# c @ ada_w moved from TensorE tiles into VectorE sums inside the two feed-forwards

## What is computed

```python
c_act = jax.nn.silu(c)                                  # c: [1, 1024]
for l in range(2):
    mod = c_act @ ada_w[l] + ada_b[l]                   # ada_w[l]: [1024, 6144]
    sh1, sc1, g1 = mod[:, None, 0:D], mod[:, None, D:2*D], mod[:, None, 2*D:3*D]
    sh2, sc2, g2 = ...
    h = rmsnorm(x, norm1_g[l]) * (1.0 + sc1) + sh1
    x = x + g1 * token_mix(h, ...)
    h = rmsnorm(x, norm2_g[l]) * (1.0 + sc2) + sh2
    x = x + g2 * grouped_moe(h, ...)

def swiglu(x, w_in, w_out):                             # the feed-forward of the first block
    a, b = jnp.split(x @ w_in, 2, axis=-1)
    return (jax.nn.silu(a) * b) @ w_out
```

## Time and profile before

| | |
|---|---|
| median of 3 runs | 1691.95 us (1687.12 to 1695.83) |
| the profiled execution: time | 1687.15 us |
| its span, first to last instruction | 1685.4 us |
| PE, DVE, ACT busy | 1537.0, 915.9, 722.9 us (91%, 54%, 43% of the span) |
| mean granted clock | 0.963 |
| chain that ended last | PE 77%, DVE 12%, ACT 5%, DMA 3%, issue 3% |
| DMA over the span | 401.98 MB, 239 GB/s |
| c @ ada_w on PE (L1562) | 768 records, 47.1 us busy |

### The profile page before, as it was taken

How to read it: one execution, slowest core, us unless ns; L and a number is a source line. 1 busy time by engine, 2 the same in 40 slices (tenths; PEclk the granted TensorE clock), 3 DMA queues, 4 the chain that set the end, 5 groups by cost and what they waited for, 6 DMA issues and landing times.

```text
span 1685.4 us, 25947 instructions
## 1 busy us (share of the span) xinstructions
PE 1537.0 (91%) x10264; PEld 1222.2 (73%) x10264; DVE 915.9 (54%) x1408; ACT 722.9 (43%) x1056; POOL 39.5 (2%) x95
## 2 busy tenths in 40 slices
PE   6999999899999999999599999979998959999996
PEld 6999987479998886777476655559788747665563
DVE  5554456655545555577653444364478775344434
ACT  5444344344444553353363444434355325344432
POOL 3200000000000000000100000000000010000000
PEclk9999999999999999999699999989999979999998
DMA  9555569855555448964169999975532425999994
GB/s 286 177 196 177 197 204 324 298 189 186 188 186 185 139 154 270 348 231 150 50 232 355 384 391 387 387 258 165 162 115 89 132 80 209 362 380 390 389 382 158
DMA packets 245842, 401.98 MB, mean 239 GB/s; under 512 B 6522, under 2 KB 151596, under 8 KB 245756
## 3 DMA queue, kind: packets, MB, share of 16 engines
q1 hardware_dynamic: 244792, 398.77, 68.8%
q10 hardware_dynamic: 372, 1.07, 0.2%
q0 software_dynamic: 592, 0.93, 0.2%
HBM read 399.70 MB, written 1.05 MB: 238 GB/s over the span
## 4 chain that ended last, share of the span: by engine, by line
PE 77%; DVE 12%; ACT 5%; DMA 3%; issue 3%; DVEq 0%; ACTq 0%; SPq 0%
PE bank L1333 15%; PE bank L1222 8%; PE bank L1406 8%; PE bank L1346 7%; PE bank L1418 7%; PE bank L1210 5%; PE bank L1234 5%; PE bank L1458 4%; PE bank L1447 4%; PE bank L1261 2%; DVE sb_w_lo L2118 2%; PE bank L1562 2%; DMA sb_ring<-in_w_up 2%; DMA sb_ring<-in_w_in 1%; DVE sb_w_lo L2052 1%
## 5 line engine op out<-in xcount | busy, mean ns | idle before, releaser
L2073 DVE TENSOR_TENSOR sb_w_lo<-sb_ring,sb_w_hi 128x1024 fp32r<-128x1024 f32 x128 | 151.2, 1223 | 160.0 <-ACT sb_w_hi L742 160.0
L1333 PE MATMUL bank<-sb_hT_hi,sb_w_hi 128*128 128x256 f32 x704 | 197.9, 281 | 2.6 <-DVE sb_w_lo L2061 2.1
L1333 PE MATMUL bank<-sb_hT_lo,sb_w_hi 128*128 128x256 f32 x704 | 198.9, 282 | 0.0
L1333 PE MATMUL bank<-sb_hT_hi,sb_w_lo 128*128 128x256 f32 x704 | 197.4, 280 | 0.0
L742 ACT ACTIVATE sb_w_hi<-sb_ring 128x1024 fp32r<-128x1024 f32 x128 | 128.5, 1052 | 135.8 <-PE bank L1333 121.9
L2118 DVE TENSOR_TENSOR sb_w_lo<-sb_ring,sb_moe_hi 128x1024 fp32r<-128x1024 f32 x144 | 168.7, 1221 | 25.6 <-ACT sb_moe_hi L793 23.8
L2052 DVE TENSOR_TENSOR sb_w_lo<-sb_ring,sb_proj_hi 128x1024 fp32r<-128x1024 f32 x100 | 117.9, 1221 | 90.3 <-ACT sb_proj_hi L722 90.3
L793 ACT ACTIVATE sb_moe_hi<-sb_ring 128x1024 fp32r<-128x1024 f32 x136 | 135.1, 1050 | 38.9 <-DMA sb_ring<-in_w_gate 35.0
L722 ACT ACTIVATE sb_proj_hi<-sb_ring 128x1024 fp32r<-128x1024 f32 x100 | 100.9, 1060 | 114.8 <-DMA sb_ring<-in_w_in 40.1
L1406 PE MATMUL bank<-sb_ring,sb_arena 128*64 128x256 f32 x1280 | 146.6, 382 | 0.5 <-DVE sb_by_slot L2142 0.5
L1333 PEld LDWEIGHTS bank<-sb_hT_hi,sb_w_hi 128*128 128x128 f32 x704 | 133.5, 190 | 4.2 <-DVE sb_w_lo L2061 2.5
(11 more groups left out here) (516 smaller groups left out, 2931.8 us busy)
## 6 DMA issues: line engine op xcount, KB each, us to landing
sb_ring<-in_w_up SPq DMA_DIRECT2D x64, 1024.0 KB, 8.1
sb_ring<-in_w_gate SPq DMA_DIRECT2D x64, 1024.0 KB, 8.3
sb_ring<-in_w_down SPq DMA_DIRECT2D x64, 1024.0 KB, 7.7
sb_ring<-in_ada_w SPq DMA_DIRECT2D x48, 1024.0 KB, 7.8
sb_ring<-in_w_in SPq DMA_DIRECT2D x46, 1024.0 KB, 5.5
sb_ring<-in_ffn_w_in SPq DMA_DIRECT2D x44, 1024.0 KB, 5.1
sb_ring<-in_ffn_w_out SPq DMA_DIRECT2D x22, 1024.0 KB, 4.9
sb_ring<-in_w_out SPq DMA_DIRECT2D x12, 1024.0 KB, 5.0
```

The source lines that it names most:

```text
L1333: ins = mm(bank[4 + 2 * p + b][:, jj * SEQ:(jj + 1) * SEQ], w[wp][:, k, jj * P:(jj + 1) * P], h_parts[hp][:, k, :], start=k == 0 and m == ...
L2073: ins = tt(w_lo[:, slot, c], ring[:, slot, c], w_hi[:, q % 2, c].bitcast(F32), ALU.subtract)
```

## The change

The 48 slabs leave the ring and PE's order. Each layer's 6144 columns are cut into six parts: an edge of 512 columns, four parts of 1280 (one for each loop turn), and an edge of 512. For each part DVE adds up eight products, one for each block of 128 rows of `ada_w`: `out = w_k * silu(c)_k + out`, with silu(c) as a scalar for each partition. The result still has 128 partitions to be added. That is done by PE in 24 products of 256 columns with `row_pick` (`ada_sums`), for layer 0 ahead of `mem_kv0`, for layer 1 behind feed-forward 2. Layer 0's sums are made in feed-forward 1, layer 1's in feed-forward 2.

The weights arrive in two buffers of their own (`ada_in`, 10 KB a partition each). A load for a loop part is 2 x 128 rows by 1280 columns (1.31 MB), for an edge 4 x 128 rows by 512 (1.05 MB). SP issues them between the ring's loads, and waits before each until DVE has used the buffer. Layer 1's last step moves too: `ada_turn(1)` and `modulation(1)` stand at the beginning of layer 0.

```diff
+        ada_edge = view(25600, 2, ADA_EDGE)
+        ada_loop = view(0, 4, ADA_LOOP)
+        ada_in = view(5120, 2, 2 * ADA_LOOP)
...
 # SP
+                def ada_load(g, j, i=0):
+                    if g == 0:
+                        if layer:
+                            sp.wait_ge(s["x"], 4)
+                    else:
+                        sp.wait_ge(s["ada_sum"], KC * i + (ADA_OPS * layer + KC * g + 2 * j - 2))
...
                 with sp.Fori(0, turns) as i:
                     step(i, j0)
+                    ada_load(1, 0, i)
+                    ada_load(1, 1, i)
                     step(i, j0 + 1)
+                    ada_load(1, 2, i)
+                    ada_load(1, 3, i)
                 load(pos + 3 * n - 1, down(turns - 1, j0 + 1))
+                ada_load(5, 0)
+                ada_load(5, 1)
...
 # DVE
+                def modulate(g, ks, i=0):
...
+                        if k:
+                            v.wait_ge(s["ada_sum"], KC * i + (ADA_OPS * layer + KC * g + k))
+                            ins = stt(out, w, ccol[:, k:k + 1], out, M, AD)
+                        else:
+                            ins = ts(out, w, ccol[:, 0:1], None, M)
+                        ins.then_inc(s["ada_sum"], 1)
+
+                def step(i, c, meanwhile=lambda n: None):
                     q = ffn_pos(n, "gate", c)
                     split(i, q)
+                    meanwhile(0)
                     product(i, c - 1)
+                    meanwhile(1)
                     split(i, q + 1)
+                    meanwhile(2)
                     hidden(i, c - 1)
                     split(i, q + 2)
+                    meanwhile(3)
...
                 with v.Fori(0, turns) as i:
-                    step(i, j0)
-                    step(i, j0 + 1)
+                    step(i, j0, lambda m: modulate(1, (m,), i))
+                    step(i, j0 + 1, lambda m: modulate(1, (4 + m,), i))
+                modulate(5, range(KC))
                 product(0, n - 1)
                 hidden(0, n - 1)
                 split(0, 3 * n - 1)
...
 # PE
-            def ada(l, m, out):
...
+            def ada_sums(l, out):
+
+                pe.wait_ge(s["ada_sum"], ADA_OPS * (l + 1))
+                for n, (row, half) in enumerate((4 * q + r, half) for q in range(3) for half in range(2) for r in range(4)):
...
             pe.wait_ge(s["x"], 1)
+            ada_sums(0, bank[0])
             mem_product("mem_kv0", bank[1])
...
             ffn("ffn2", n1, n1, 2)
+            ada_sums(1, bank[7])
             pe.wait_ge(s["x"], 6)
+            ada_turn(1, bank[3])
...
 # ACT
-            used(f"ada{ADA_SLABS - 1}.0")
+            act.wait_ge(s["ada_turned"], 1)
             A(ada_rows, bank[0][:, :], ACT.Copy).then_inc(s["ada_rows"], 1)
 
             norm(next(roots), "x", 3, lambda half: ffn_begin("ffn2", (half,)))
             turn_parts(4, gain("ffn2"))
             ffn("ffn2", n1, n1)
+            act.wait_ge(s["ada_turned"], 3)
+            A(ada_rows, bank[7][:, :], ACT.Copy).then_inc(s["ada_rows"], 1)
```

More of the change, by code:

```diff
@@ L49 @@
 ADA = 6 * D
[L50 to L53, removed]
+ADA_LOOP, ADA_EDGE = 1280, 512
+ADA_OPS = 6 * KC
 ARENA = 27200
@@ L101, in build @@
         scol = sb("scol", [P, LAYERS, 2, KC])
-        cpick = sb("cpick", [P, 12 + 32 * KC])
+        ccol = sb("ccol", [P, KC])
+        row_pick = sb("row_pick", [P, 12 + 32])
         group_sum = sb("group_sum", [P, NE])
@@ L388, in build @@
         tiles_used = sem("tiles_used")
+        ada_full = [sem(f"ada_full{n}") for n in range(2)]
         block = ctx.enter_context(nc.Block())
@@ L1552, in sparse @@
                 pe.sem_inc(s["acc_half"], 1)
-            def ada(l, m, out):
-                pos = place[f"ada{m}.{l}"]
-                landed(pos)
-                w = slot_view(pos, FB)
-                row, half = m // 2, m % 2
-                for k in range(KC):
-                    g = 32 * (k % 4)
-                    ins = mm(out[g:g + 32, half * FB:(half + 1) * FB], cpick[:, 12 + 32 * k - row:44 + 32 * k - row], w[:, k, :],
-                             start=m == 0 and k < 4, stop=m >= ADA_SLABS - 2 and k >= 4, skip_group_check=True)
-                ins.then_inc(tiles_used, 1)
+            def ada_sums(l, out):
+                pe.wait_ge(s["ada_sum"], ADA_OPS * (l + 1))
+                for n, (row, half) in enumerate((4 * q + r, half) for q in range(3) for half in range(2) for r in range(4)):
+                    g = 32 * (row % 4)
+                    m = 2 * row + half
+                    ins = mm(out[g:g + 32, half * FB:(half + 1) * FB], row_pick[:, 12 - row:44 - row], ada_cols(m),
+                             start=n < 4, stop=n >= 16, skip_group_check=True)
+                ins.then_inc(s["ada_turned"], 1)
             def ada_turn(l, out):
@@ L1798, in _ @@
                         by_token(f"gates{n}.{l}", bank[n % 3], hT_lo_l)
-                    if l == 0:
-                        for m in range(ADA_EACH[1] * n, ADA_EACH[1] * (n + 1)):
-                            ada(1, m, bank[3])
                     if n == 0:
@@ L1837, in _ @@
                 ins.then_inc(s["hg_o"], 1)
-                if l == 0:
-                    ada_turn(1, bank[3])
                 pe.wait_ge(s["gates"], 8 * l + 8)
@@ L2395, in _ @@
                     link(ins)
[L2396 removed]
+            ins.then_inc(s["mix_step_dve"], 1)
             used("w_in4")
@@ L2485, in _ @@
                 split(tiles[1])
+                if l == 0:
+                    modulation(1)
                 for n in range(2, 9):
```

109 lines of the change are left out of this document (51 added, 58 removed).

## The result

| | before | after |
|---|---|---|
| median, same session | 1690.63 us (4 runs) | 1676.76 us (4 runs, 1675.35 to 1677.44) |
| ratio of the runs | | 0.9914, 95% interval 0.9887 to 0.9942 |
| the profiled execution: time, span | 1687.15, 1685.4 us | 1677.24, 1675.5 us |
| PE, DVE, ACT busy | 1537.0, 915.9, 722.9 us | 1505.3, 1024.6, 722.8 us |
| mean granted clock | 0.963 | 0.953 |

What follows compares the result with a forecast made beforehand. PE was taken to bound the feed-forward loops, with room on DVE and DMA. Terms -27.1 - 7 + 17.4 + 4.3 + 0.6 = -11.8 us took the median of 1691.95 to 1680, range 1666 to 1698.

Steps and rivals of the forecast that it cites:

- Layer 0, -27.1: Second block, kv_up to `br_b`: without slabs layer 0 takes layer 1's 82.05 us instead of 109.2, saving 27.1 us.
- The mix, -7: First block's mix: removing 24 slabs, partly in PE's gaps, gives -10 us, less 3 for a lower clock: -7.
- (a): Mix: seven slabs ahead of the end of `w_in7`, for which DVE waits, go away: -8.4 us.
- (b): Mix: layer 0's `ada_sums` now stands ahead of `mem_kv0`, 24 products on PE: +2.8 us.
- (c): Mix: ACT's split of `w_in2` waits for small DVE operations and comes later than PE needs it: +1.3 us.
- (g): Mix: without slabs as fillers PE idles longer before the attention's transposes, which with the scores run at half clock: +3 us.
- The loop, 0: Feed-forward loops: DVE's eight sums a turn at 1.55 us and the added loads fit beside PE, 1.2 us slack: no loss.
- Rival (1): DMA binds the feed-forward loops, so the kernel is slower or the same, 1693 to 1707 us; chance 0.13.
- Rival (2): DVE binds the feed-forward loops, a sum taking 2.9 us: +48 us in eight turns, 1728; chance 0.04.
- The ends, +17.4: End of each feed-forward: last edge's sums delay the last down tile, PE stalls 6.7 us plus 2 for clock; twice, +17.4.
- Rival (3): Feed-forward ends stall less, 4.3 us each without cold clock, as the load lands under the first sums: 1671 us; chance 0.12.
- (4): Rival: the mix's slabs only filled waits, so mix gains 0, with end stalls of 10 + 2 each: 1694 us; chance 0.11.

Runs made afterwards that it cites:

- experiment 1: Changed kernel with all eight sums of each feed-forward's last edge moved behind the split of tile 32: 1653.85 us, ratio 0.9781 to the kernel before.
- experiment 8: Two kernels, each the changed kernel with unused extra sums in feed-forward 1 and unused extra loads in feed-forward 2: 1685.88 and 1699.36 us, one run each.
- the second trace: The changed kernel run once more without any edit, for another trace of the same program: 1672.78 us (one run).
- experiment 5: Changed kernel with layer 0's 24 slabs put back into the first block's mix and no sums or loads in feed-forward 1: 1677.17 us, ratio 0.9938.
- experiment 8, second kernel: Changed kernel with a second sum at all eight places of a turn in feed-forward 1, one spare load a turn in feed-forward 2: 1699.36 us (one run).
- experiment 8's first kernel: Changed kernel with one extra sum per loop step in feed-forward 1 and two spare loads a turn in feed-forward 2: 1685.88 us (one run).

## Why the prediction was right, point by point

- **Layer 0, -27.1.** kv_up to `br_b` fell from 109.2 to 84.3 us, 24.8, and 1.5 more fell away between the transposes and kv_up, where no slab had stood. In the profiled execution 8 us behind kv_up ran at a mean clock of 0.79; experiment 1 had 1.00 there. The comparison with layer 1 was the right yardstick, and the yardstick moved. In the same trace layer 1 takes 84.3 us too, where it took 82.05 before:

```profile
1204.67 4.45 PE L1284 MATMUL bank<-sb_ring,sb_arena 128*128 128x512 f32 x10
...
1293.44 0.72 PE L1257 MATMUL bank<-sb_proj_hi,sb_ymT_hi 128*128 128x512 f32 x2 [3.04 <-DVE sb_ymT_lo L2690]
```

  With experiment 1's clock layer 0 took 83.4, so about 1.0 us of the 2.3 missing ones is the clock; the cause of the other 1.3 is open.
- **The mix, -7.** Start of the norm to the transposes: 80.81 before, 76.87 after, -3.9; forecast (a) + (b) + (c) = -4.3. (b) `ada_sums(0)` took 2.8. (c) an idle of 1.17 us at `w_in2`, 1.3 forecast. The attention gave 1.1 (1.4), the `w_out` tiles and the copy 3.6 (4.3). The clock, (g): from the transposes to the scores 5.24 us instead of 3.73, +1.5, half of the 3 that I took. Half clock further on in the attention is part of the 1.1 above.
- **The loop, 0.** Right, with more room than I saw: the sum's 1.55 us was exact, but the order had at least 1.55 us of slack left where I had 1.2, and DMA gave 390 and not 360. The error is in the slack: I set only 0.86 us of waiting against ACT's delay, though in the kernel after ACT still stands 3.11 us waiting for PE in such a step:

```profile
189.68 2.02 ACT L766 ACTIVATE sb_w_hi<-sb_ring 128x1024 fp32r<-128x1024 f32 x2 [3.11 <-PE bank L1356]
```

  Rival (1) was to decide from 341 GB/s down; the loop ran at 343 and, in experiment 8, at 385 without a loss. Rival (2) needed sums of over 2.1 us; they take 1.55.
- **The ends, +17.4, with the first edges +18.0.** 9.56 and 7.25, 16.8; in the second trace 9.56 and 9.13, 18.7. Idle 6.87 for 6.7; the load landed at 199.8 (5.2 us) for 199.6; the last down tile took 8.0 us instead of 5.6 (207.68 to 215.65), 2.4 for my 2. This was the term that decided the size, and experiment 1 shows that it belongs to the placing of eight sums, not to the idea.
- **ACT's order, +4.3.** 3.8.
- **The rest.** I had none in the sum; +3.9 in one trace, -1.2 in the other.
- Rival (3) fails on the landing time, (4) on experiment 5. Forecast -11.8, profile to profile -9.9, medians -13.9.
- The terms and their places were right. That the total came so near is in part luck: layer 0 gave 2.3 us less between kv_up and `br_b` and 1.5 more ahead of it, which no term held, and the rest moved by 3.9 one way or 1.2 the other.

## What to carry over

Work can be moved free of cost to an engine that has room in a loop, as long as it stays inside the loop; what doesn't fit into the turns must not stand ahead of the last instructions that the bound engine waits for. Look at the epilogue first: the placing of the last edge alone was worth 18 to 23 us here, more than the change itself gained. When a term rests on PE's clock behind idles of 2 to 5 us, carry it as a range: two executions of one program differed by 2.6 us in one stage, and layer 1's mix, whose code no edit touches, took 235.0 us in one trace and 240.3 in another (experiment 8, second kernel), with half clock granted at one place behind its beginning and at four.

## What the runs showed of the hardware

- A product with a column scalar and a sum, fp32, all operands in SBUF: 482 ns for 256 columns, 744 for 512, 1545 for 1280; queued ones start 1.46 us apart at 1280.
- Loads of 1 KB, 4 KB and 5 KB rows on one queue moved 390 GB/s together, with median landings of 11 to 15 us in feed-forward 2 of experiment 8's first kernel, against 7 to 10 at 343 GB/s. Up to 385 PE saw nothing of it.
- Behind an idle of 1.30 us the granted clock stayed at 1.00, behind 6.87 us it was 0.50 for the next 4 us; behind 2.41 us it was 1.00 or a mean of 0.72 over six us, and behind 4.50 us 0.50 or 0.72, in two executions of the same program.
